# A hybrid decoder trunk on one core: gates and branch outputs with tokens on the partitions, and the modulation sections' sums in the norms' waits

## The chip, the cores and the metric

The kernel runs on 1 core of one Trainium2 chip. The metric is the device time of one execution in microseconds, as the median of several runs. Engines are called TensorE (PE, with its weight loads as PEld), VectorE (DVE), ScalarE (ACT), GpSimd (POOL) and SyncE (SP).

## The reference

256 tokens (T) of 1024 channels (D) pass two layers, in float32. A conditioning vector gives each layer six *sections* of modulation (shift, scale and gate for either half of the layer). Cut to what matters:

```python
mod = (silu(c) @ ada_w[l] + ada_b[l])            # six sections of D
sh1, sc1, g1, sh2, sc2, g2 = jnp.split(mod, 6, axis=-1)
h = rmsnorm(x, norm_mix_w[l]) * (1 + sc1) + sh1
proj = h @ w_in                                   # nine groups of 512, three gates of 1024
y_a = short_conv_mixer(a_b, a_c, a_h, conv_w) @ w_br_a
y_b = hgrn2_mixer(b_q, b_f, b_i, b_g, lb, hgrn_norm_w) @ w_br_b
y_c = chunked_sgu(c_u, c_v, sgu_norm_w, sgu_w, sgu_b) @ w_br_c
merged = sigmoid(gate_a)*y_a + sigmoid(gate_b)*y_b + sigmoid(gate_c)*y_c
x = x + g1 * (merged @ w_o)
h = rmsnorm(x, norm_ffn_w[l]) * (1 + sc2) + sh2
x = x + g2 * (swiglu(h) if l == 0 else top2_of_8_experts(h))
```

A final RMSNorm follows.

## The kernel before, in words

Activations stand with channels on the partitions: `xT`, `hS` (the normed input, split in two), `merged` are 128 x 8 chunks x 256 tokens. Every float32 product is made of three fp32r matmuls. Each operand is split into a high part (a copy rounded to fp32r) and a low part (the rest); high x high, high x low and low x high are added in PSUM (`tile`, L664 is the one matmul call).

**Weights** come in pieces of 512 KB, in the fixed order of the list `PIECES` (`dense_pieces`, L177). SyncE loads piece after piece into `raw`, a ring of 11 slots; a slot is loaded again when VectorE has read it. ScalarE writes the high part of a piece into `split`, a ring of 6 (`high_parts`, L1212), VectorE the low part (`low_parts`, L1447), and TensorE then uses it. Both engines keep some pieces ahead, and each splits the pieces that are due *before* it turns to its next other step: `unit(key)` does so up to a bound, then waits for TensorE's result.

**Sections.** A section is 1024 x 1024 weights, eight pieces that aren't split. VectorE multiplies each with its part of `silu(c)` and adds it into an accumulator (`product`, L1522 and L1525); a product frees its slot of `raw`. TensorE sums the accumulator over the partitions with eight products of one column (`ada_sum`), which is called a section sum, and VectorE adds the bias (`modulate`, L1533). `ADA_ORDER` is the order of the sections, number 6 x layer + part.

**PSUM.** Four banks `psU` go round among the *units* (`UNITS`: one bank each of a projection, gate, branch output), four banks `psA` in pairs among the *events* (`EVENTS`: norm sums, section sums, scores). TensorE opens a unit when the one four before it is emptied, an event when the one two before it is.

**A layer.** Norm 1; the nine groups of projections (`HEAD_GROUPS`) with the recurrence's levels between them; then for each branch, in the order a, c, b: four gate units, four output units. A gate unit holds 2 channel tiles x 256 tokens and takes 48 matmuls of 256 columns with two pieces, an output unit 24 with one. ScalarE takes the sigmoid (L1321) and copies the branch's input into `yS` (high part); VectorE multiplies with the output and adds into `merged` (L1865 to L1871) and makes the low parts. Then the output projection `wo`, the residual add (L1884), and norm 2: ScalarE squares, TensorE sums them over the partitions (`stat_sum`, `stat_pair`), ScalarE takes the root, VectorE the reciprocal (L1559), and chunk after chunk of the next `hS` (L1565, L1276, L1652). In the waits of the norms TensorE does section sums and *fills* (`stream`: products whose result nobody reads, 6 of 256 columns before the dense layer and before layer 1, 2 before the router). Layer 0 goes on with the dense SwiGLU (11 pairs of tiles, then the down product), layer 1 with the router and the experts.

Of the sections, one is summed after branch a in each layer (2 and 8), three in the loop of the dense layer (5, 6, 7), the rest in the norms' waits.

Of the kernel before, what the change touches and what calls it, by code (L numbers as in the profile page):

```python
# [50 lines left out]
BRANCHES = ["a", "c", "b"]  # L51

# [24 lines left out]
ADA_ORDER = [0, 1, 2, 3, 4, 5, 6, 7, 11, 8, 9, 10]  # L77
FFN_ADA = [5, 6, 7]
DOWN_ADA = [11]
# [4 lines left out]
FFN_TAKE = [3, 3, 2] * 3 + [0, 0]  # L84
assert sum(FFN_TAKE) == KD * len(FFN_ADA)

FFN_SUMS = {next(p for p in range(NF // 2) if sum(FFN_TAKE[:p + 1]) >= KD * (n + 1)) + 1: s
            for n, s in enumerate(FFN_ADA)}

# [9 lines left out]
FILL_NORM, FILL_LOGITS = 6, 2  # L99
# [3 lines left out]
def unit_plan():  # L103

    plan = [("c", "D")] + [(("x", j), "A") for j in range(4)] + [(("vec", 0), "A")]
    for l in range(DEPTH):
# [4 lines left out]
        for b in BRANCHES:  # L111
            plan += [((l, "gate" + b, j), "A") for j in range(4)]
            plan += [((l, "y" + b, j), "D") for j in range(4)]
        plan += [((l, "wo", j), "D") for j in range(4)]
        if l == 0:
            plan += [(("ffn", j), "D") for j in range(NF)] + [(("mod", s), "D") for s in DOWN_ADA]
# [6 lines left out]
def event_plan():  # L123

    plan = []
    for l in range(DEPTH):
# [6 lines left out]
        plan += [(("ada", 6 * l + s), "D") for s in (2, 4)]  # L133
        plan += [((l, "norm2"), "A"), (("ada", 6 * l + 3), "D")]
        if l == 0:
            plan += [(("ada", s), "D") for s in FFN_ADA]
            plan += [("down0", "D"), ("down1", "D")]
# [10 lines left out]
def unit_signals():  # L148
# [6 lines left out]
    for key, _ in UNITS:  # L155
# [4 lines left out]
        elif kind in ("i", "v", "ffn"):  # L160
            used += 4 if key[-1] % 2 == 0 else 0
            signal[key] = ("used", used, used)
        elif kind in HEAD_GROUPS or kind in ("gatea", "gateb", "gatec", "wo", "ya", "yb", "yc"):
            used += 1 if kind[0] == "y" else 2
            signal[key] = ("used", used, used)
        else:
            direct += 1
            used += NF if kind == "mod" else 0
# [8 lines left out]
def dense_pieces():  # L177
# [22 lines left out]
    for l in range(DEPTH):  # L200
        for g in HEAD_GROUPS:
# [6 lines left out]
            if g == "f":  # L208
                two = section()
            if g == "f" and l:  # L210
                out += two[:4]
            if g == "ab" and l == 0:
                out[-2:] = two[:2] + out[-2:] + two[2:4]
            if g == "u":
# [7 lines left out]
        out += [("split", "w_o", l, q * 512, 256 * j, 256) for j in range(4) for q in range(2)]  # L222
# [1962 lines left out]
```

## Time and profile before

| | us |
|---|---|
| median of 3 runs (lowest, highest) | 1528.2 (1528.18, 1531.08) |
| the profiled execution | 1528.13 |
| its span in the trace | 1526.2 |
| TensorE busy | 1509.5 (99%) |
| VectorE busy | 1297.7 (85%) |
| ScalarE busy | 958.4 (63%) |

Layer 0's branches lie at about 156 to 264 us of the span, its dense layer at 292 to 489, layer 1's branches at 621 to 729; the experts begin at 768. TensorE's busy time counts pipelined matmuls whose ends are modelled, so 99% says that it seldom stands still, and nothing of how fast it goes; the spacing of matmuls says that. Where TensorE waits, the timeline names the engine that released it.

### The profile page before, as it was taken

How to read it: one execution, taken by the hardware profiler on the slowest of the kernel's cores; microseconds unless marked ns; L12 is line 12 of the kernel's file. 1: busy time of each engine (PE TensorE's matmuls, PEld its weight loads, DVE VectorE, ACT ScalarE, POOL GpSimd, SP SyncE). 2: the span in 40 equal slices, each digit the busy share in tenths (PEclk: the TensorE clock that was granted, in tenths of full speed). 3: DMA queues.
4: the chain of work that ended last, by engine and by line, in shares of the span. 5: the costliest groups of instructions: out<-in, count | busy, mean ns of one | idle time of the engine just before them, and what ended most of it. 6: DMA issues, size and time to landing. Idle time of an engine off the chain costs nothing.

```text
span 1526.2 us, 26183 instructions
## 1 busy us (share of the span) xinstructions
PE 1509.5 (99%) x9449; PEld 1363.4 (89%) x9449; DVE 1297.7 (85%) x1492; ACT 958.4 (63%) x1103; POOL 29.3 (2%) x45
## 2 busy tenths in 40 slices
PE   8999999999999999999999999999999999999997
PEld 7999999999999999999988888888888888888886
DVE  7997788787764788778699999999999999999998
ACT  3535444544543534544498887878878888888785
POOL 0000000000000000000010000000000000000100
PEclk9999999999999999999999999999999999999999
DMA  9946589388996644778389999999999999999993
GB/s 350 332 148 201 187 276 317 111 279 289 367 383 241 208 138 153 239 263 300 110 323 395 410 394 404 381 368 412 366 384 378 379 410 357 393 372 381 410 393 141
DMA packets 228897, 471.01 MB, mean 309 GB/s; under 512 B 16156, under 2 KB 130004, under 8 KB 228820
## 3 DMA queue, kind: packets, MB, share of 16 engines
q1 hardware_dynamic: 225056, 457.27, 82.9%
q0 software_dynamic: 3488, 12.59, 2.1%
q8 instruction: 51, 0.84, 0.2%
q14 instruction: 26, 0.21, 0.0%
q10 hardware_dynamic: 276, 0.09, 0.0%
HBM read 454.69 MB, written 15.21 MB: 308 GB/s over the span
## 4 chain that ended last, share of the span: by engine, by line
PE 94%; DVE 3%; DMA 1%; ACT 0%; issue 0%; SPq 0%; DVEq 0%; ACTq 0%
PE psU L664 68%; PE psA L664 24%; DMA raw<-in_ada_w_dram 1%; DVE split L1954 1%; PE psA L1113 1%; PE psU L1073 0%; PE psU L1026 0%; ACT split L1212 0%; SPq L497 0%; DVE work L1474 0%; DVE work L1484 0%; DVE adacc L1586 0%; DVE adacc L1589 0%; DVE merged L1611 0%; DVE masks L1489 0%
## 5 line engine op out<-in xcount | busy, mean ns | idle before, releaser
L1212 ACT ACTIVATE split<-raw 128x1024 fp32r<-128x1024 f32 x750 | 783.6, 1061 | 358.2 <-PE psU L664 177.3
L1954 DVE TENSOR_TENSOR split<-raw,split 128x1024 fp32r<-128x1024 f32 x528 | 617.0, 1220 | 22.8 <-ACT split L1212 10.6
L664 PE MATMUL psU<-split,yS 128*128 128x512 f32 x2112 | 485.0, 390 | 0.1
L664 PE MATMUL psU<-hS,split 128*128 128x256 f32 x3840 | 470.7, 284 | 2.6 <-DVE hS L1652 2.6
L664 PEld LDWEIGHTS psU<-hS,split 128*128 128x128 f32 x3840 | 464.7, 192 | 4.8 <-DVE split L1447 2.7
L664 PEld LDWEIGHTS psU<-split,yS 128*128 128x128 f32 x2112 | 395.0, 188 | 81.9 <-DVE split L1954 0.7
L1447 DVE TENSOR_TENSOR split<-raw,split 128x1024 fp32r<-128x1024 f32 x222 | 265.0, 1219 | 68.1 <-ACT split L1212 67.4
L664 PE MATMUL psA<-split,hidE 128*128 128x512 f32 x1056 | 246.0, 392 | 0.0
L664 PEld LDWEIGHTS psA<-split,hidE 128*128 128x128 f32 x1056 | 196.4, 188 | 40.2
L1525 DVE SCALAR_TENSOR_TENSOR adacc<-raw,cact,adacc 128x1024 f32<-128x1024 f32 x56 | 71.8, 1282 | 3.6 <-DVE adacc L1525 0.5
L664 PE MATMUL psU<-yS,split 128*128 128x256 f32 x576 | 70.1, 283 | 0.0
L664 PEld LDWEIGHTS psU<-yS,split 128*128 128x128 f32 x576 | 69.6, 192 | 0.0
L664 PE MATMUL psA<-hid_hi,split 128*128 128x256 f32 x352 | 63.9, 284 | 0.3 <-DVE mod L1533 0.3
L664 PEld LDWEIGHTS psA<-hid_hi,split 128*128 128x128 f32 x352 | 55.0, 192 | 0.5 <-DVE mod L1533 0.5
L664 PE MATMUL psU<-split,hS 128*128 128x512 f32 x192 | 45.1, 392 | 0.0
L664 PEld LDWEIGHTS psU<-split,hS 128*128 128x128 f32 x192 | 35.6, 188 | 7.2
L2110 DVE TENSOR_TENSOR hidE<-psA,hidE 128x512 fp32r<-128x512 f32 (+1 forms) x48 | 29.5, 642 | 14.6 <-ACT hidE L1212 14.6
L1321 ACT ACTIVATE sig<-psU 128x512 f32<-128x512 f32 x24 | 14.2, 592 | 38.6 <-PE psU L664 38.6
L1212 ACT ACTIVATE hidE<-psA 128x512 fp32r<-128x512 f32 (+1 forms) x48 | 25.2, 560 | 17.8 <-PE psA L1113 17.8
L664 PE MATMUL psA<-hid,split 128*128 128x256 f32 x128 | 36.2, 283 | 0.0
L2103 DVE TENSOR_TENSOR sig<-sig,psU 128x512 f32<-128x512 f32 (+1 forms) x48 | 29.3, 638 | 6.6 <-PE psU L664 6.6
L664 PE MATMUL psA<-work 128*128 128x128 f32 x272 | 33.3, 275 | 0.0
(255 smaller groups left out, 836.3 us busy)
## 6 DMA issues: line engine op xcount, KB each, us to landing
raw<-in_moe_w_dram SPq DMA_DIRECT2D x496, 512.0 KB, 5.8
raw<-in_w_in_dram SPq DMA_DIRECT2D x116, 512.0 KB, 5.5
raw<-in_ada_w_dram SPq DMA_DIRECT2D x96, 512.0 KB, 7.8
raw<-in_ffn_w_dram SPq DMA_DIRECT2D x66, 512.0 KB, 8.1
raw<-in_moe_w_dram SPq DMA_DIRECT2D x64, 256.0 KB, 6.4
raw<-in_w_o_dram SPq DMA_DIRECT2D x16, 512.0 KB, 8.4
token_rows<-sc SPq DMA_DIRECT2D x11, 512.0 KB, 12.2
raw<-in_w_br_a_dram SPq DMA_DIRECT2D x8, 512.0 KB, 9.2
```

The lines of the kernel that those rows point to most:

```text
L664: return pe.matmul(o, a, b, start=start, stop=stop, skip_group_check=True)
L1113: last = pe.transpose(T_BANKS[g % 2][:, m * CAP:(m + 1) * CAP], sig[0:CAP, 2 + g % 2, m * P:(m + 1) * P], ident[0:CAP, 0:CAP])
L1212: return act.activation(o, i, ACT.Copy)
L1321: act.activation(sig[:, j, :], bank[:, :], ACT.Sigmoid).then_inc(s_uA, 1)
L1447: TTN(split[:, n % SPL, 1, :], raw[:, SPLIT_POS[n] % RAW, :], split[:, n % SPL, 0, :].bitcast(F32), ALU.subtract).then_inc(s_lo, 1)
L1525: STT(acc, raw[:, pos % RAW, :], cact[:, k:k + 1], acc, ALU.mult, ALU.add).then_inc(s_afree, 1)
L1954: TTN(split[:, slot, 1, :], raw[:, (RAW0 + n) % RAW, :], split[:, slot, 0, :].bitcast(F32), ALU.subtract).then_inc(s_lo, 1)
L2103: TTN(sig[0:CAP, 2 + g % 2, 0:width], s, three, ALU.mult).then_inc(s_hrow, 1)
L2110: TTN(h_lo, T_BANKS[g % 2][:, 0:len(tiles) * CAP], h_hi.bitcast(F32), ALU.subtract).then_inc(s_hlo, 1)
```

## The change

Four things. (1) Gates and branch outputs are computed with tokens on the partitions: a unit is 128 tokens x 512 channels, h (or the branch's input) is the stationary operand and the weights are the moving one, 512 columns a matmul (`half_rows`). Two units (the two token tiles) share four pieces for a gate, two for an output, and gate halves and output halves take turns. (2) `merged` then has tokens on the partitions, and TensorE turns it back, 4 x 4 transposes of 128 x 128 (`turn_merged`), before the output projection; ScalarE and VectorE read the turned rows from the spare banks of two events. The branch input for branch a is split earlier, in the head, and for the others when the previous branch's last output is done. (3) Each branch has one section beside it (4, 3, 5 of the layer), the dense loop two (6, 7; two products a pair), the down product one (8), layer 1's head none; three more accumulators. (4) Each norm's wait has three section sums in place of fills (one fill stays before the dense layer), and norm 1 of layer 1 sums the squares on VectorE first, as norm 2 did.

```diff
+WO_ORDER = [(0, 0), (1, 0), (0, 1), (1, 1), (2, 0), (2, 1), (3, 0), (3, 1)]
-ADA_ORDER = [0, 1, 2, 3, 4, 5, 6, 7, 11, 8, 9, 10]
-FFN_ADA = [5, 6, 7]
-DOWN_ADA = [11]
+ADA_ORDER = [0, 1, 2, 4, 3, 5, 6, 7, 8, 10, 9, 11]
+BRANCH_ADA = [4, 3, 5]
+FFN_ADA = [6, 7]
+DOWN_ADA = [8]
+NORM_SUMS = [7, 6, 8]
-FFN_TAKE = [3, 3, 2] * 3 + [0, 0]
+FFN_TAKE = [2] * 8 + [0] * 3
-FILL_NORM, FILL_LOGITS = 6, 2
+FILL_NORM = 1
...
         for b in BRANCHES:
-            plan += [((l, "gate" + b, j), "A") for j in range(4)]
-            plan += [((l, "y" + b, j), "D") for j in range(4)]
+            for hh in range(2):
+                plan += [((l, "gate" + b, 2 * hh + tt), "A") for tt in range(TT)]
+                plan += [((l, "y" + b, 2 * hh + tt), "D") for tt in range(TT)]
...
         for b in BRANCHES:
-            gates = [("split", "w_in", l, q * 512, GATE0[b] + 256 * j, 256) for j in range(4) for q in range(2)]
-            ada = section() if b != BRANCHES[0] else []
-            for q, gate in enumerate(gates):
-                out += [gate] + ada[q:q + 1]
-            out += [("split", "w_br_" + b, l, 0, 256 * j, 256) for j in range(4)]
+            ada = section()
+            for hh in range(2):
+                for q in range(4):
+                    out += [("split", "w_in", l, q * 256, GATE0[b] + 512 * hh, 512)] + ada[4 * hh + q:4 * hh + q + 1]
+                out += [("split", "w_br_" + b, l, q * 256, 512 * hh, 512) for q in range(2)]
...
+            def half_rows(banks, nq, x):
+
+                for q in range(nq):
+                    w = next_split()
+                    for tt in range(TT):
+                        for kk in range(2):
+                            for wp, hp in ((0, 0), (1, 0), (0, 1)):
+                                last = mm(banks[tt][:, :], x[:, hp, 2 * q + kk, tt * P:(tt + 1) * P],
+                                          w[wp][:, kk * 512:(kk + 1) * 512], (q, kk, wp, hp) == (0, 0, 0, 0),
+                                          (q, kk, hp) == (nq - 1, 1, 1))
+                    last.then_inc(s_used, 1)
+
+            def turn_merged(l, i, bank):
+
+                pe.wait_ge(s_mg, 8 * l + 4 + 2 * (i // 2) + 2)
+                if i > 1:
+                    pe.wait_ge(s_ml, 4 * l + i - 1)
...
+                        last = pe.transpose(bank[:, m * T + tt * P:m * T + (tt + 1) * P], row[:, col:col + P], ident[:, :])
...
                 for n, b in enumerate(BRANCHES):
+                    for hh in range(2):
+                        half_rows([open_unit((l, "gate" + b, 2 * hh + tt)) for tt in range(TT)], 4, hS)
+                        if (n, hh) == (2, 1):
+                            stat, spare1 = open_event((l, "norm2"))
+                            scale, spare0 = open_event(("ada", 6 * l + 4))
+                            turn_merged(l, 0, spare0)
+                            turn_merged(l, 1, spare1)
+                        banks = [open_unit((l, "y" + b, 2 * hh + tt)) for tt in range(TT)]
+                        if hh == 0:
                             pe.wait_ge(s_yl, 3 * l + n + 1)
+                        half_rows(banks, 2, yS)
+                    if n == 0 and l == 0:
+                        ada_sum(2)
...
+                        if (j, q, m) == (1, 0, 1):
+                            turn_merged(l, 2, spare0)
+                            turn_merged(l, 3, spare1)
...
-                stat_sum(stat, l)
-                ada_sum(6 * l + 4, scale)
+                stat_sum(stat, 2 * l)
+                ada_sum(6 * l + 4, scale, range(5))
                 stat_pair(stat, 2 * l + 2, 3)
+                ada_sum(6 * l + 4, scale, range(5, KD))
                 ada_sum(6 * l + 3)
+                ada_sum(6 * l + 5)
...
-                    if pair in FFN_SUMS:
-                        ada_sum(FFN_SUMS[pair])
...
-                        stat_pair(stat, 3, 0)
...
+                scale = open_unit(("mod", NORM_SUMS[0]))
+                ada_sum(NORM_SUMS[0], scale, range(5))
+                stat_sum(stat, 1).then_inc(s_used, 1)
+                stat_pair(stat, 3, 3)
+                ada_sum(NORM_SUMS[0], scale, range(5, KD))
+                for s in NORM_SUMS[1:]:
+                    ada_sum(s)
...
+            def branch_high(l, n):
+
+                act.wait_ge(s_y, 3 * l + n + 1)
+                src = {"a": AH, "c": UB, "b": YB}[BRANCHES[n]]
+                copy(yS[:, 0, :, :].rearrange("p a b -> p (a b)"), src).then_inc(s_yh, 1)
...
                 for n, b in enumerate(BRANCHES):
+                    if n:
+                        act.wait_ge(s_used, SIGNAL[l, "y" + BRANCHES[n - 1], 3][1])
+                        branch_high(l, n)
...
+                    gates = SIGNAL[(l, "gate" + BRANCHES[n], 0)][2] - 4
                     for k in ks:
-                        if n:
-                            low_parts(gates + k + 1)
-                        product(6 * l + 2 + n, k)
+                        low_parts(gates + k + (5 if k < 4 else 6))
+                        product(6 * l + BRANCH_ADA[n], k)
...
                     if n:
-                        ada_part(n, range(4))
                         branch_low(n)
-                        ada_part(n, range(4, KD))
+                    ada_part(n, range(4))
                     for j in range(4):
+                        if j == 2:
+                            ada_part(n, range(4, KD))
+                        if (n, j) == (2, 2):
+                            merged_low(0)
+                            merged_low(1)
```

How the order moves on the engines, in three places. First **ScalarE, at the start of branch b in layer 0, before** (`yS` is the branch's input, `split<-raw` the high part of a weight piece, `sig` a gate's sigmoid; `pieceN_loaded` names the slot of `raw`):

```order
L1321 ACTIVATE sig<-psU2 128x512 [waits merged_ready,pieces_used]
L1212 ACTIVATE yS<-work 128x1024 [waits branch_input_ready]
L1212 ACTIVATE split<-raw 128x1024 [waits pieces_used,piece3_loaded]
L1212 ACTIVATE split<-raw 128x1024 [waits pieces_used,piece5_loaded]
L1321 ACTIVATE sig<-psU3 128x512 [waits merged_ready,pieces_used]
```

The same place under the change:

```order
L1244 ACTIVATE yS<-work 128x1024 [waits branch_input_ready,pieces_used]
L1244 ACTIVATE split<-raw 128x1024 [waits pieces_used,piece1_loaded]
L1244 ACTIVATE split<-raw 128x1024 [waits pieces_used,piece3_loaded]
L1244 ACTIVATE split<-raw 128x1024 [waits pieces_used,piece5_loaded]
L1244 ACTIVATE split<-raw 128x1024 [waits pieces_used,piece6_loaded]
L1244 ACTIVATE split<-raw 128x1024 [waits pieces_used,piece7_loaded]
L1244 ACTIVATE split<-raw 128x1024 [waits pieces_used,piece9_loaded]
L1244 ACTIVATE split<-raw 128x1024 [waits pieces_used,piece0_loaded]
L1369 ACTIVATE sig<-psU2 128x512 [waits merged_ready,pieces_used]
L1369 ACTIVATE sig<-psU3 128x512 [waits merged_ready,pieces_used]
```

The branch's input is copied first, and seven pieces (the last two in slots 9 and 0) stand ahead of the two sigmoids, where two stood ahead of the second.

**VectorE, at the same place under the change**, from the last output of branch c on (`sig<-sig,psU` is gate times output, `merged<-merged,sig` the sum, `yS` the low part of the input, `work<-raw,cact` a section product):

```order
L1914 TENSOR_TENSOR sig<-sig,psU 128x512 [waits act_unit_emptied,pieces_used]
L1918 TENSOR_TENSOR merged<-merged,sig 128x512 [waits dve_unit_emptied]
L1857 TENSOR_TENSOR yS<-work,yS 128x1024 [waits branch_input_high]
L1491 TENSOR_TENSOR split<-raw,split 128x1024 [waits act_high_parts]
L1565 TENSOR_SCALAR work<-raw,cact 128x1024 [waits piece9_loaded]
L1491 TENSOR_TENSOR split<-raw,split 128x1024 [waits act_high_parts]
L1568 SCALAR_TENSOR_TENSOR work<-raw,cact,work 128x1024 [waits ada_products,piece0_loaded]
```

The two products read slots 9 and 0, which are loaded again for the last two of ScalarE's seven pieces. Before, the first four products stood ahead of `yS`.

**TensorE, norm 2 of layer 0, before** (`sig,ones` are the sums of squares, `ones,work` and `ones,adacc` section sums, `sgub,ones` fills):

```order
L664 MATMUL psU<-hS,split 128x256 x192
L664 MATMUL psA<-sig,ones 128x256
L664 MATMUL psA<-ones,work 128x1 x8
L664 MATMUL psA<-sig,ones 128x256 x2
L664 MATMUL psA<-ones,adacc 128x1 x8
L664 MATMUL psU<-sgub,ones 128x256 x6
```

And under the change, from the transposes after the last gates of branch b on:

```order
L743 MATMUL psA<-ident,merged 128x128 x8
L672 MATMUL psU<-split,yS 128x512 x24
L672 MATMUL psU<-hS,split 128x256 x36
L743 MATMUL psA<-ident,merged 128x128 x8
L672 MATMUL psU<-hS,split 128x256 x156
L672 MATMUL psA<-sig,ones 128x256
L672 MATMUL psA<-ones,work 128x1 x5
L672 MATMUL psA<-sig,ones 128x256 x2
L672 MATMUL psA<-ones,work 128x1 x3
L672 MATMUL psA<-ones,adacc 128x1 x8
L672 MATMUL psA<-ones,work 128x1 x8
L672 MATMUL psU<-sgub,ones 128x256
```

Eight transposes stand inside the last branch and eight after 36 matmuls of the output projection; the first section sum is cut 5 + 3 around the last squares, and a third sum takes the place of five fills.

## Rows read from the trace of the kernel before

**Rows 1.** The page's chain that ended last: share of the span by engine.
```profile
PE 94%; DVE 3%; DMA 1%; ACT 0%; issue 0%; SPq 0%; DVEq 0%; ACTq 0%
```

**Rows 2.** That chain in order of time: start us, us, what ran.
```profile
107.76 10.89 PE psU L664 x48
...
190.54 1.68 PE psA L664 x16
192.22 72.09 PE psU L664 x600
```

**Rows 3.** Timeline, start of the down product: start, us, engine, operation, idle before.
```profile
424.94 0.36 PE L664 MATMUL psA<-hid_hi,split 128*128 128x256 f32 x1 [0.31 <-DVE mod L1533]
```

**Rows 4.** Timeline, norm 2 of layer 0.
```profile
285.69 0.63 ACT L1266 ACTIVATE sig<-xT 128x512 f32<-128x512 f32 x1 [2.67 <-DVE xT L1884]
...
286.69 0.73 PEld L664 LDWEIGHTS psA<-sig,ones 128*128 128x128 f32 x4
...
287.09 0.17 DVE L1542 SCALAR_TENSOR_TENSOR wm<-mod,vecs 128x8 f32<-128x8 f32 x1
287.45 1.97 PEld L664 LDWEIGHTS psA<-ones,adacc 128*128 128x128 f32 x16
...
288.37 1.75 DVE L1559 RECIPROCAL rstd<-rstd 128x256 f32<-128x256 f32 x1 [1.11 <-ACT rstd L1230]
289.34 2.46 PEld L664 LDWEIGHTS psU<-sgub,ones 128*128 128x128 f32 x12
...
291.96 4.15 PEld L664 LDWEIGHTS psU<-hS,split 128*128 128x128 f32 x31 [0.17 <-DVE hS L1652]
```

**Rows 5.** Timeline, norm 1 of layer 1: sums of the first and the last squares.
```profile
486.09 0.74 PEld L664 LDWEIGHTS psA<-sig,ones 128*128 128x128 f32 x4
...
491.00 0.73 PEld L664 LDWEIGHTS psA<-sig,ones 128*128 128x128 f32 x4 [0.30 <-ACT sig L1266]
```

**Rows 6.** Timeline, norm 2 of layer 1, up to the router's first matmul.
```profile
751.47 0.73 PEld L664 LDWEIGHTS psA<-sig,ones 128*128 128x128 f32 x4
...
754.04 1.38 PEld L1026 LDWEIGHTS psU<-ident,xT 128*128 128x128 f32 x12
...
756.50 3.65 PEld L664 LDWEIGHTS psU<-rtw,merged 128*128 128x128 f32 x32 [0.38 <-ACT merged L1276]
```

**Rows 7.** Timeline, start of branch b in layer 0 (SPq issues the loads).
```profile
228.25 0.75 DVE L1522 TENSOR_SCALAR work<-raw,cact 128x1024 f32<-128x1024 f32 x1
229.03 0.37 SPq L497 DMA_DIRECT2D raw<-in_w_in_dram  x1
...
230.41 0.37 SPq L497 DMA_DIRECT2D raw<-in_w_in_dram  x1
...
232.93 1.06 ACT L1212 ACTIVATE split<-raw 128x1024 fp32r<-128x1024 f32 x1 [4.89 <-DMA raw<-in_w_in_dram]
233.89 0.58 ACT L1321 ACTIVATE sig<-psU 128x512 f32<-128x512 f32 x1
...
236.58 1.06 ACT L1212 ACTIVATE split<-raw 128x1024 fp32r<-128x1024 f32 x1 [1.17 <-DMA raw<-in_w_in_dram]
```

**Rows 8.** Timeline of VectorE: product to product with one low part; multiply to low part.
```profile
206.63 1.28 DVE L1525 SCALAR_TENSOR_TENSOR adacc<-raw,cact,adacc 128x1024 f32<-128x1024 f32 x1
...
208.97 1.28 DVE L1525 SCALAR_TENSOR_TENSOR adacc<-raw,cact,adacc 128x1024 f32<-128x1024 f32 x1
...
259.14 0.68 DVE L1867 TENSOR_TENSOR sig<-sig,psU 128x512 f32<-128x512 f32 x1
...
260.46 0.68 DVE L1851 TENSOR_TENSOR hS<-merged,hS 128x512 fp32r<-128x512 f32 x1
```

**Rows 9.** The page's DMA issues: the longest median landing of raw weights.
```profile
raw<-in_w_br_a_dram SPq DMA_DIRECT2D x8, 512.0 KB, 9.2
```

**Rows 10.** TensorE after its longest stop: timeline, then the stretch's busy times, granted clock.
```profile
41.09 7.17 PE L664 MATMUL psU<-hS,split 128*128 128x256 f32 x45 [2.56 <-DVE hS L1652]
...
41.10:46.00 4.90, 4.90 (x28) 4.90 (x29) 4.88 (x8) 4.41 (x6) 0.00 (x0) 0.65 0.97 283
```

More of the change, by code:

```diff
@@ L167, in unit_signals @@
             direct += 1
[L168 removed]
+            used += NF if key == ("mod", NORM_SUMS[0]) else 0
             signal[key] = ("direct", direct, used)
@@ L452, in program, with accumulator, sum_before @@
         s_yfirst = sem("expert_first_half_ready")
+        def accumulator(s):
+            return accs.get(s, adacc[:, :])
+        def sum_before(s):
+            same = {4: [4, 10], 5: [5, 11], 0: [6], 1: [7]}.get(s % 6 if s not in (6, 7) else s - 6)
+            same = same or [t for t in ADA_ORDER if t != 1 and t not in accs]
+            return same[same.index(s) - 1] if same.index(s) else None
         block = ctx.enter_context(nc.Block())
@@ L712, in project_rows @@
                         yield q // 2
+            def half_rows(banks, nq, x):
[12 more added lines that the diff above has]
+                    pe.wait_ge(s_ml, 4 * l + i - 1)
+                for m in range(2):
+                    col = (2 * i + m) % 4 * P
+                    for tt in range(TT):
+                        row = merged[:, 4 * (i // 2) + 2 * tt:4 * (i // 2) + 2 * tt + 2, :].rearrange("p a b -> p (a b)")
+                        last = pe.transpose(bank[:, m * T + tt * P:m * T + (tt + 1) * P], row[:, col:col + P], ident[:, :])
+                last.then_inc(s_mt, 1)
             def stat_pair(bank, count, j):
@@ L870, in chunk @@
                 def chunk(k):
-                    if l and k == 0:
-                        stream(psU[(units[0] - 1) % 4], FILL_NORM)
                     pe.wait_ge(s_h, 2 * KD * l + k + 1)
@@ L892, in mixer @@
                 for n, b in enumerate(BRANCHES):
-                    for gg in range(2):
-                        for _ in project(lambda j: (l, "gate" + b, 2 * gg + j)):
-                            pass
-                    for j in range(4):
-                        bank = open_unit((l, "y" + b, j))
-                        if j == 0:
-                            pe.wait_ge(s_yl, 3 * l + n + 1)
-                        w = next_split()
-                        for m in range(2):
-                            for k in range(4):
-                                last = tile(bank[:, m * T:(m + 1) * T], w, k, k * 256 + m * P,
-                                            m == 0 and k == 0, k == 3, yS)
-                        last.then_inc(s_used, 1)
-                    if n == 0:
-                        ada_sum(6 * l + 2)
+                    for hh in range(2):
[7 more added lines that the diff above has]
+                        if hh == 0:
+                            pe.wait_ge(s_yl, 3 * l + n + 1)
+                        half_rows(banks, 2, yS)
+                    if n == 0 and l == 0:
+                        ada_sum(2)
                 def chunk_m(k):
@@ L1033, in _ @@
             bank = open_unit("logits")
-            stream(bank, FILL_LOGITS)
             for k in range(KD):
@@ L1514, in product @@
                 dve.wait_ge(s_raw[pos % RAW], 16 * (pos // RAW + 1))
[L1515 removed]
+                acc = accumulator(s)
                 if k == 0:
[L1517 to L1520 removed]
+                    last = sum_before(s)
+                    if last is not None:
+                        dve.wait_ge(*((s_unit, SIGNAL["mod", last][1]) if last in NORM_SUMS else
                                       (s_ev, EVENT_AT[("ada", last) if last else ("half", 1)] + 1)))
@@ L1722, in mixer @@
                     modulate(DOWN_ADA[0])
-                    for k in range(4):
-                        product(6 * l + 2, k)
-                        if k % 2 == 0:
-                            low_parts(SIGNAL[l, "f", 0][2] + 3 + k // 2)
                 else:
@@ L1802, in mixer @@
                 dve.wait_ge(s_eD, emptied(EVENTS, EVENT_AT[(l, "sgu")], "D"))
-                for k in range(4, KD):
-                    product(6 * l + 2, k)
+                for k in range(4, KD) if l == 0 else ():
+                    product(2, k)
                     if k == 5:
@@ L1914, in _ @@
                     for _ in range(FFN_TAKE[pair]):
-                        if done % KD == 0 and done:
-                            modulate(FFN_ADA[done // KD - 1])
                         product(FFN_ADA[done // KD], done % KD)
```

157 lines of the change are left out of this document (77 added, 80 removed).

## The prediction

> **What bounds the kernel now.** I read the chain that ended last first: 94% of the span is TensorE, and the line names only its matmuls with any weight [rows 1]. So an edit counts by what it takes from or adds to TensorE's stream; other engines count only where TensorE would wait for them. Then the chain in order of time, for rates. Narrow matmuls (256 columns) come at 72.09 / 600 = 120.2 ns, wide ones (512) at 10.89 / 48 = 226.9 ns, and one section sum (8 fp32 products of one column, 16 passes) inside the stream costs 1.68 us [rows 2]. Third, the timeline where that stream breaks: the waits before a norm's first result [rows 4 to 6] and the bank wait ahead of the down product, 0.31 us [rows 3]. Last, the hand-over from one branch to the next, because the slots of raw weights, ScalarE and VectorE meet there [rows 7, 8]. Outside these places TensorE never stops.
>
> All sums are against the profiled execution, 1528.13 us (span 1526.2); the median of the runs, 1528.2, is the same number. About 0.2% (3.1 us) is what a measurement of this kernel can tell from no change.
>
> **The change, part by part.**
>
> 1. Wide form. Per layer, 3 branches x (192 + 96) = 864 narrow matmuls become 432 wide ones: 864 x 120.2 = 103.8 us against 432 x 226.9 = 98.0 us, 5.8 us less, so **-11.6 us** for two layers. The weight loads hide under the matmuls in both rates. The wide rate is measured on the same shape (h tile stationary, weights moving), so I take it as it stands. The rows show 12 to 13 ns of cost per matmul beside its columns (2 x 120.2 - 226.9 = 13.5). The Trainium skill, "TensorE: Matmul & The Clock Gate", section "Back-to-back issue gap", puts that fixed part at about 2.5 ns; by it 864 fewer matmuls would give 2.2 us, not 11.6, and the whole sum would be 1530.2. Rows 2 contradict it for this kernel's fp32r matmuls.
>
> 2. Turning the merged rows back. 16 transposes a layer; 12 of this kind load in 1.38 us [rows 6], so 16 x 0.115 = 1.84 us: **+3.7 us** for both layers. The first 8 read banks long finished. The other 8 wait for the last merged sums: after the last branch product VectorE does two pairs of multiply and add (1.32 us each [rows 8]), started 1.3 us late by the weight halves it must do first: ready at 3.95 us. TensorE meanwhile has 36 output-projection matmuls, 4.33 us. Hidden, but with 0.4 us to spare; if the cover fails it costs what VectorE is late. Cost 0, bounds 0 and +2 us a layer.
>
> 3. Sums taken out of the stream. Sections 5, 6, 7 (in the dense layer's loop) and 8 (after the first branch of layer 1) leave it: 4 x 1.68 = **-6.7 us**. The loop's last modulation, for which the down product waited, goes too: **-0.3 us** [rows 3].
>
> 4. The three waits they move into. *Norm 2, layer 0* [rows 4]. T is the load of the last squares' sum. Squares end at 286.32, but T was 286.69, behind a whole section sum; with 5 of its 8 products ahead T is 0.3 us earlier. Then three products follow T by 0.76 us and end near T+1.75, the scale's two small VectorE steps after them, and the reciprocal starts at T+2.15 instead of T+1.68. First result usable 0.47 us later: T+5.74 instead of T+5.27. TensorE: the next sum needs the bank that ScalarE's root empties (T+1.7), two sums at 1.89 (287.45 to 289.34), one fill 0.41: T+5.9. Net **+0.3 us**. *Norm 1, layer 1* [rows 5]: 0.77 us of squares' sums leaves the down product, but the new VectorE sum of squares stands ahead of the last residual add and gives only 0.35 of it back; the reciprocal's 0.4 us delay takes that. **0**; bounds -0.8 and +0.8. *Norm 2, layer 1* [rows 6]: here the router, not a matrix product, follows. Before, its first matmul came at T+5.03. Now TensorE is busy to T+5.48 and then turns 3 tiles (1.38 us): T+6.86, less the 0.3 of T: **+1.5 us**, since routing, gather and the first expert queue up behind it. Bounds 0 (the first expert's splitting hides it) and +1.8.
>
> 5. More sections beside the branches. The queue to follow is ScalarE's. Before, it made two weight halves ahead of a gate's sigmoid at a branch's start; now it makes seven, the last two from slots that VectorE's first and second section product free (the rows of its order under the change). TensorE needs the first gate bank again after six pieces, 72 x 0.227 = 16.3 us. Branch b, times from its first matmul: ScalarE copies the branch input and two halves, done 2.2 and 3.2; VectorE's two low parts to 4.5, its two late pairs for the previous branch (1.32 each) to 7.1, the branch's low part and one more to 9.4, first product 0.75 to 10.2, next low part and product 2.34 to 12.5 [rows 7, 8]. SyncE refills the two slots at 10.2 and 12.5. In rows 7 such refills were usable 3.9 us (first) and 6.2 us (third) after issue; this is the third in its queue with more room, so 4.5: 17.1. Half 1.06, sigmoid 0.58: 18.7. TensorE waits **2.4 us** (1.8 at 3.9, 4.1 at 6.2). Branch c of layer 1: the previous outputs need only the multiply, 1.4 us less, so 1.0 us. Branch c of layer 0: TensorE has the section sum (1.68) first, 0. Branch a has no late outputs: 0. Total 2 x 2.4 + 1.0 = **+5.8 us**; bounds 0 (if VectorE's queue runs 2.4 us ahead of this) and +24 (a landing of 9.2 us [rows 9] each time: 7.1 + 7.1 + 5.7 + 4.1).
>
> Fewer products in the dense loop (2 a pair instead of 3) cost nothing and gain nothing: TensorE does not wait there [rows 1, 2].
>
> Sum: -11.6 + 3.7 - 6.7 - 0.3 + 0.3 + 0 + 1.5 + 5.8 = -7.3: **1520.8 us**.
>
> **Rivals.**
>
> *B, the gates are in time.* Term 5 is 0: 1528.1 - 13.1 = 1515.0. For it: 2.4 us is one or two VectorE instructions of margin in a chain of ten. Against: every link of it has a row.
>
> *C, the clock falls in the norms' waits.* Once in this trace TensorE idled 2.56 us, and the granted clock over the next 4.9 us was 0.65, a mix of 2.4 and 1.2 GHz: 4.9 x 0.35 = 1.7 us lost [rows 10]. Fills held it at 1.00 in the norms; now one-column sums stand there for about 4 us on end. If each wait pays 1.7 us: 1520.8 + 5.1 = 1525.9. Against: before, too, two of the three waits were mostly such sums, and TensorE is seldom idle in them. The Trainium skill, same page, section "What's actually happening", says that the default state is throttled and activity releases it; it does not say whether one column is activity.
>
> *D, slower: the ring of raw weights becomes the bound.* Eight products now stand in all three branches, and all weights pass one ring of 11 slots that VectorE frees in order. If each refill takes the 9.2 us of rows 9 instead of 4.5, TensorE waits 24 us at the four hand-overs: 1528.1 - 13.1 + 24 = 1539. The new time passes the old one once these waits exceed 13.1 us, some 3.3 us each. For it: ScalarE already waited 4.89 us for such a refill. Against: that was with rows of 1 KB; gate and branch weights now come in rows of 2 KB.
>
> *E, the wide form is no cheaper:* one wide matmul takes as long beside the branches as two narrow ones, 240.4 ns, because h and the branch inputs are now the weights that are loaded. Term 1 is 0: 1520.8 + 11.6 = 1532.4. Against: rows 2 show the form with h as weights at 226.9 ns. The page named under 1 points the same way, with its own figure.
>
> **How the numbers follow.** A (forecast) 0.48, with its own range 1517 to 1525; B 0.22; C 0.13; D 0.14, of which half stops short of the full price; E 0.03. Faster by over 0.2% (below 1525.1): A 0.46, B 0.22, C 0.07, D 0.03 = 0.78. Within 0.2%: A 0.02, C 0.06, D 0.05, E 0.01 = 0.14. Slower (above 1531.3): D 0.06, E 0.02 = 0.08. The range 1513.5 to 1527.5 takes B with most of term 4's lower bounds, A and C, and leaves out most of D and E, under 0.2.
>
> **What would show it.** Wide matmuls in the branches at 227 ns; no section sum in the dense loop; 8 + 8 transposes a layer of 0.9 us each without a wait before the second 8; the first residual matmul after norm 2 of layer 0 near T+5.9; the router's first near T+6.9; and at branch b, in both layers, TensorE idle about 2.4 us before the third gate bank, released by a ScalarE sigmoid. No such idle time means B; a granted clock under 1.00 after the norms means C; longer waits at every hand-over with ScalarE waiting for raw weights mean D. I am wrong altogether if a wait appears inside the output projection or if the first expert does not move with the router.

## The result, and the profile after

The changed kernel takes 1547.9 us in the median against 1528.6 us for the kernel before on the same chip: 1.0113 times as long, 95% interval 1.0095 to 1.0132. The forecast was 1520.8, faster. It is slower, by 17 us as the ratio and the two profiled executions have it (19 between the medians), and outside the range.

| | before, us | after, us |
|---|---|---|
| the profiled execution | 1528.13 | 1545.23 |
| its span | 1526.2 | 1543.4 |
| TensorE busy | 1509.5, 9449 matmuls | 1510.5, 8581 matmuls |
| TensorE waiting for ScalarE's sigmoids | 0 | 15.3 |
| mean granted clock | 0.998 | 0.985 |

868 matmuls fewer, and the same busy time: what was saved came back as slow matmuls. The rest is standstill: all of TensorE's waits sum to 25.5 us after the change and to 9.6 before. The three rows of these waits that matter (line, waited for: us in total, times, longest):

```profile
PE psU L672 <- ACT sig L1369: 15.3, 5, 4.1
PE psA L672 <- ACT sig L1298: 0.9, 3, 0.6
PE psU L672 <- DVE hS L1698: 2.6, 1, 2.6
```

L1369 is the gate sigmoid. Nothing like the first row was there before; the third was, with the same 2.6 us. The waits stand in both layers, in branch a (4.11 and 3.91 us), branch b (2.59 and 3.36) and branch c of layer 1 (1.35). TensorE around branch a and branch b of layer 0 (start, us, engine, operation, idle before):

```profile
166.34 5.60 PE L672 MATMUL psU<-split,yS 128*128 128x512 f32 x24
176.06 12.78 PE L672 MATMUL psU<-split,hS 128*128 128x512 f32 x48 [4.11 <-ACT sig L1369]
...
228.60 11.04 PE L672 MATMUL psU<-split,hS 128*128 128x512 f32 x48
239.48 5.60 PE L672 MATMUL psU<-split,yS 128*128 128x512 f32 x24
247.67 12.79 PE L672 MATMUL psU<-split,hS 128*128 128x512 f32 x48 [2.59 <-ACT sig L1369]
260.29 1.03 PE L743 MATMUL psA<-ident,merged 128*128 128x128 f32 x8
```

Two things are to be seen. The 48 wide matmuls take 11.04 us where TensorE comes to them running, and 12.78 behind each of these two stops: such a wait costs 1.7 us more than its length. (Behind the 3.91 us of layer 1 they take 13.65, behind the 1.35 of branch c 11.16.) And the undisturbed 48 come at the forecast rate: (239.48 - 228.60) / 48 = 226.7 ns.

Why the sigmoid of branch a is late, read from the three other queues (SPq issues the loads of raw weights):

```profile
151.38 3.35 DVE L1872 RECIPROCAL work<-work 128x512 f32<-128x512 f32 x1 [1.82 <-ACT work L1262]
...
155.73 3.34 DVE L1874 RECIPROCAL work<-work 128x512 f32<-128x512 f32 x1
...
165.88 0.75 DVE L1565 TENSOR_SCALAR work<-raw,cact 128x1024 f32<-128x1024 f32 x1
```

```profile
166.66 0.37 SPq L505 DMA_DIRECT2D raw<-in_w_in_dram  x1
...
168.05 0.37 SPq L505 DMA_DIRECT2D raw<-in_w_in_dram  x1
```

```profile
158.44 1.06 ACT L1244 ACTIVATE split<-raw 128x1024 fp32r<-128x1024 f32 x1 [1.26 <-PE psU L672]
170.68 1.06 ACT L1244 ACTIVATE split<-raw 128x1024 fp32r<-128x1024 f32 x1 [11.17 <-DMA raw<-in_w_in_dram]
173.93 1.06 ACT L1244 ACTIVATE split<-raw 128x1024 fp32r<-128x1024 f32 x1 [2.19 <-DMA raw<-in_w_in_dram]
174.89 1.06 ACT L1369 ACTIVATE sig<-psU 128x512 f32<-128x512 f32 x2
```

The branch's first matmul was at 155.44. VectorE was still in the mixer's own steps, two reciprocals among them, and began its first section product only at 165.88, 10.4 us in. Layer 1 has the same steps and the same 10.4 us. That product frees the slot for a load issued at 166.66, usable at 170.68; the next, issued at 168.05, is usable at 173.93. ScalarE's order puts both halves ahead of the sigmoid.

Now the clock. Norm 2 of layer 0, which answers to [rows 4]:

```profile
290.51 0.59 PE L672 MATMUL psA<-sig,ones 128*128 128x256 f32 x2
290.94 1.17 PE L672 MATMUL psA<-ones,work 128*128 128x1 f32 x10
292.31 1.13 PE L672 MATMUL psA<-sig,ones 128*128 128x256 f32 x4 [0.19 <-ACT sig L1298]
293.27 0.72 PE L672 MATMUL psA<-ones,work 128*128 128x1 f32 x6
294.09 1.92 PE L672 MATMUL psA<-ones,adacc 128*128 128x1 f32 x16
295.87 3.03 PE L672 MATMUL psA<-ones,work 128*128 128x1 f32 x16
298.76 1.20 PE L672 MATMUL psU<-sgub,ones 128*128 128x256 f32 x2
```

The last section sum takes 3.03 us where the one ahead of it takes 1.92, and the fill's two matmuls 1.20. The windows of the same stretch, and of the router's wait in layer 1 (window, length, busy us and count of PE, PEld, DVE, ACT, POOL; then the granted clock of TensorE, DMA share, GB/s):

```profile
178.00:182.00 4.00, 4.00 (x14) 3.21 (x13) 4.00 (x5) 1.87 (x2) 0.00 (x0) 0.70 0.99 363
182.00:186.00 4.00, 4.00 (x20) 3.29 (x19) 4.00 (x5) 1.87 (x3) 0.00 (x0) 1.00 0.97 327
...
294.00:298.00 4.00, 3.91 (x29) 3.94 (x29) 3.93 (x9) 2.19 (x4) 0.00 (x0) 0.81 0.03 8
298.00:302.00 4.00, 4.00 (x18) 3.82 (x18) 4.00 (x11) 2.55 (x6) 0.00 (x0) 0.50 0.00 0
302.00:306.00 4.00, 4.00 (x31) 4.00 (x31) 2.28 (x5) 1.06 (x1) 0.00 (x0) 0.84 0.00 0
...
770.00:774.00 4.00, 4.00 (x20) 4.00 (x21) 2.94 (x15) 3.28 (x8) 0.00 (x0) 0.50 0.21 76
```

0.50 is the lower level, 1.2 GHz. PE is "busy" 4.00 of 4.00 us there, so the busy column hides the loss; the count does not (18 matmuls in 4 us against 31). From the start to the last matmul, window length times (1 - clock) sums to 20.5 us after and to 1.7 us before. Of the 20.5, 8.5 lie in and behind the sigmoids' waits, 10.2 in and behind the three norms' waits, and 1.7 behind the 2.56 us stop at 41 us, which the kernel before has too. (In every run the clock falls once more after the last matmul, where TensorE has nothing left to do; that is not counted.)

Where the 17.1 us of span came from, in us by stage, each from its first matmul (the first from the span's start) to that of the next:

| stage | before | after | difference | forecast |
|---|---|---|---|---|
| mixer of layer 0, up to norm 2 | 284.58 | 290.51 | +5.9 | -1.6 |
| norm 2's wait | 7.39 | 8.89 | +1.5 | +0.3 |
| dense gate and up products | 132.97 | 128.61 | -4.4 | -5.4 |
| down product and norm 1 | 71.42 | 71.62 | +0.2 | 0 |
| mixer of layer 1 | 253.01 | 262.40 | +9.4 | -2.2 |
| norm 2 of layer 1, up to the router | 7.13 | 11.26 | +4.1 | +1.5 |
| router to the first expert | 11.49 | 11.88 | +0.4 | 0 |
| experts and output | 758.2 | 758.2 | 0 | 0 |

### The profile page after: what moved, and what is told of

Read it like the earlier page. It is cut to its first block and busy times, and to the rows that moved or that the text cites. A ratio compares the mean times of both kernels' runs of the same rounds, so it can differ in the third digit from the quotient of the medians.

```text
span 1543.4 us, 24440 instructions
## 1 busy us (share of the span) xinstructions
PE 1510.5 (98%) x8581; PEld 1328.5 (86%) x8581; DVE 1295.4 (84%) x1495; ACT 956.8 (62%) x1103; POOL 29.2 (2%) x45
## 5 line engine op out<-in xcount | busy, mean ns | idle before, releaser
L2002 DVE TENSOR_TENSOR split<-raw,split 128x1024 fp32r<-128x1024 f32 x528 | 617.2, 1222 | 22.8 <-ACT split L1244 10.4
L672 PE MATMUL psU<-split,yS 128*128 128x512 f32 x2400 | 552.4, 390 | 0.1
L672 PEld LDWEIGHTS psU<-split,yS 128*128 128x128 f32 x2400 | 449.1, 188 | 92.9 <-DVE split L2002 0.7
L672 PE MATMUL psU<-hS,split 128*128 128x256 f32 x2688 | 334.0, 287 | 2.6 <-DVE hS L1698 2.6
L672 PEld LDWEIGHTS psU<-hS,split 128*128 128x128 f32 x2688 | 329.5, 195 | 4.0 <-DVE split L1491 2.7
L672 PE MATMUL psU<-split,hS 128*128 128x512 f32 x768 | 185.8, 403 | 15.3 <-ACT sig L1369 15.3
L672 PEld LDWEIGHTS psU<-split,hS 128*128 128x128 f32 x768 | 148.5, 195 | 48.6 <-ACT sig L1369 17.3
L1957 DVE TENSOR_TENSOR sig<-sig,psU 128x256 f32<-128x256 f32 x22 | 9.1, 418 | 33.8 <-ACT sig L1386 33.8
L1568 DVE SCALAR_TENSOR_TENSOR adacc<-raw,cact,adacc 128x1024 f32<-128x1024 f32 x28 | 35.9, 1281 | 0.7
L1568 DVE SCALAR_TENSOR_TENSOR work<-raw,cact,work 128x1024 f32<-128x1024 f32 x28 | 35.8, 1279 | 0.2
L1386 ACT ACTIVATE sig<-psU 128x256 f32<-128x256 f32 x22 | 8.3, 380 | 41.7 <-PE psU L672 41.7
```

Source lines behind the costliest of these rows:

```text
L672: return pe.matmul(o, a, b, start=start, stop=stop, skip_group_check=True)
L1386: act.activation(sig[:, f % 4, 0:T], bank[:, 0:T], ACT.Silu).then_inc(s_sig, 1)
L1568: STT(acc, raw[:, pos % RAW, :], cact[:, k:k + 1], acc, ALU.mult, ALU.add).then_inc(s_afree, 1)
L1957: TTN(sig[:, f % 4, T:2 * T], sig[:, f % 4, 0:T], bank[:, T:2 * T], ALU.mult).then_inc(s_uD, 1)
L2002: TTN(split[:, slot, 1, :], raw[:, (RAW0 + n) % RAW, :], split[:, slot, 0, :].bitcast(F32), ALU.subtract).then_inc(s_lo, 1)
```

## The experiments

Theory 1: TensorE's waits for the sigmoids, with the clock that each takes down, are one half of the loss. Theory 2: section sums of one column, standing in the norms' waits, let the clock fall, and that is the other half. The rivals stand in the expectations. All ratios are to the kernel before, on the same chip; "us" of gain below are differences of these ratios, and each such difference is good to about 4 us.

| kernel | median, us | ratio (95% interval) |
|---|---|---|
| the change | 1547.9 | 1.0113 (1.0095 to 1.0132) |
| e1_sigmoid_early | 1537.1 | 1.0051 (1.0034 to 1.0069) |
| e2_wide_sums | 1537.7 | 1.0054 (1.0039 to 1.0068) |
| e3_both | 1528.4 | 0.9992 (0.9980 to 1.0004) |
| e4_narrow_fills | 1535.5 | 1.0035 (1.0017 to 1.0053) |
| e6_branch_a_early | 1543.4 | 1.0079 (1.0053 to 1.0104) |
| e5_second_rows_first | 1523.4 | 0.9958 (0.9941 to 0.9974) |
| e8_y_lows_first | 1524.0 | 0.9963 (0.9950 to 0.9977) |

### e1_sigmoid_early

```
# ScalarE, unit(key), gate keys
-    upto = min(upto, SIGNAL[key[0], key[1], 3][2] + 4)
+    upto = used + 3
```

> The changed kernel with one number altered: before the sigmoid of a gate unit ScalarE makes only the split pieces up to three past that unit, no longer seven. Theory (the stalls and the clock they take with them are the loss): no TensorE wait on the sigmoids is left (15.3 us in five places in the changed kernel), the clock rows at 176, 248, 640 and 712 us of the changed kernel are back at 1.00 (8.5 us), the three norm waits stay as they are; 1547.9 - 23.8 = about 1524 us. Rival 1 (pieces made late instead): the splits that now come after the sigmoid reach TensorE late, the stall moves to the weight loads that wait on ScalarE's split, and the time stays at 1540 or above. Rival 2 (the token-major form itself, its transposes or its traffic is what costs): the stalls go and the time stays near 1548.

Measured: 0.0062 of the ratio came back, 9.5 us, not 24. The larger of TensorE's waits:

```profile
PE psA L743 <- DVE merged L1918: 4.0, 2, 2.0
...
PE psU L672 <- DVE split L1491: 2.7, 5, 0.6
...
PE psU L672 <- DVE hS L1893: 1.5, 2, 0.7
```

The sigmoids' 15.3 us are gone, and so are the clock's falls in the branches. In their place stand 8.2 us of other waits: 4.0 ahead of the second transposes, 2.7 on low parts of weights, 1.5 on the merged rows' low parts. The lost time had been hiding lateness of VectorE. So 15.3 - 8.2 = 7.1 us of standstill are gone, and with the falls in the branches 8.5 us of clock. But the fall at the router in layer 1 is now twice as long:

```profile
760.00:768.00 8.00, 8.00 (x40) 8.00 (x39) 1.19 (x12) 0.88 (x2) 0.00 (x0) 0.50 0.00 0
```

The clock's loss up to the last matmul is 15.4 us against 20.5. By stages of the two profiled executions (9.4 us apart), the mixers take 12.2 us less, the norms and the dense layer 0.8 less, and router to first expert 3.6 more (15.46 us against 11.88). (The mixers' 12.2 is some 3 us short of what standstill and clock lost there less; that is not assigned.) Why that fall grew is not shown: the instructions there are the same.

Theory 1 holds in its mechanism and fails in its price: 24 took the standstills as if nothing queued up behind them. Rival 2 is out, since the time did not stay. Rival 1 has a small part of the truth. Three of the five waits on low parts (0.64 us each) go back to ScalarE. The rows are those ahead of TensorE's wait at 226.83; the first wait is for branch c's last product:

```profile
223.51 1.06 ACT L1244 ACTIVATE yS<-work 128x1024 fp32r<-128x1024 f32 x1 [4.35 <-PE psU L672]
...
225.55 3.50 DVE L1491 TENSOR_TENSOR split<-raw,split 128x1024 fp32r<-128x1024 f32 x3 [2.60 <-ACT split L1244]
```

### e2_wide_sums

```
# ada_sum: column k of the bank is the same sum; the columns behind it are overwritten by k + 1, ...
-    last = mm(bank[:, k:k + 1], acc[:, k * P:(k + 1) * P], ones[:, 0:1], True, True)
+    last = mm(bank[:, k:k + P], acc[:, k * P:(k + 1) * P], ones[:, :], True, True)
```

> The changed kernel with every section sum's matmul given a moving operand of 128 columns in place of one (column k of the bank holds the same sum; the loads of weights, which set the pace, stay). Theory (the clock falls in the norms' waits because what stands there is matmuls of one column): granted clock 1.00 in the slices that hold the three norm waits, the same waits in number and order, about 8 to 10 us less; 1538 to 1540 us. Rival (the clock falls because TensorE waits there, whatever the width): slices stay at 0.5 to 0.8, time stays 1548 within 2 us, or more if the wider matmuls take longer than their loads.

Measured: 9.0 us less. Norm 2 of layer 0 and its windows:

```profile
294.93 0.83 PE L672 MATMUL psA<-ones,work 128*128 128x128 f32 x6
295.75 2.02 PE L672 MATMUL psA<-ones,adacc 128*128 128x128 f32 x16
297.61 1.95 PE L672 MATMUL psA<-ones,work 128*128 128x128 f32 x16
299.40 0.60 PE L672 MATMUL psU<-sgub,ones 128*128 128x256 f32 x2
```

```profile
294.00:298.00 4.00, 4.00 (x30) 3.75 (x31) 2.73 (x6) 1.42 (x2) 0.00 (x0) 1.00 0.32 107
298.00:302.00 4.00, 4.00 (x34) 3.90 (x33) 4.00 (x11) 2.69 (x6) 0.00 (x0) 1.00 0.01 2
...
766.00:770.00 4.00, 4.00 (x38) 4.00 (x37) 2.85 (x15) 2.98 (x7) 0.00 (x0) 1.00 0.13 51
```

The same instructions in the same order, 128 columns in place of one: a sum of 16 passes starts 1.86 us ahead of the next instruction instead of 1.78, and the clock stays at 1.00 in all three waits, also in norm 1 of layer 1, where TensorE still stops for 0.56 and 0.53 us. The sigmoids' waits are as they were (16.2 us). Theory 2 is shown, and the rival (TensorE's waiting is what counts, not the width) is out. The two profiled executions are 7.4 us apart, a little less than the ratios.

### e3_both

Both edits.

> Both edits together: no wait on the sigmoids and 128-column section sums. Theory: the two effects are apart and add: 1547.9 - 23.8 - 9 = about 1515 us, below the kernel before. Rival: the two share what they gain, and the time is no better than the better of the two alone (about 1524).

Measured: 0.9992, equal to the kernel before. The two effects add (9.5 + 9.0 = 18.5; measured 0.0121, 18.5 us) as far as 4 us of uncertainty can tell. The level is 13 us above the 1515 written down: the new waits below are 9.7 us, and the clock's two falls in the branches 3.4.

```profile
PE psU L672 <- DVE split L1491: 4.2, 6, 0.9
PE psA L743 <- DVE merged L1918: 4.0, 2, 2.0
...
PE psU L672 <- DVE hS L1893: 1.5, 2, 0.8
```

Its clock still falls twice, behind the 0.8 and 2.0 us waits of each layer. In e1_sigmoid_early the same pairs of waits (0.74 and 2.02, 0.74 and 2.01 us) were followed by no fall, so their length alone does not decide it. In this kernel the norms run at full clock, so it shows term 4 undisturbed: from the first squares' sum to the first residual product 7.5 us in layer 0 (before 7.4), to the router 8.5 in layer 1 (before 7.1).

### e4_narrow_fills

```
# the kernel before, stream(): the fills in the norms' and the router's waits
-    for _ in range(count):
-        mm(bank[:, 0:T], ones[:, :], sgub[:, 0, 0:2, :].rearrange("p g t -> p (g t)"), True, True)
+    for _ in range(2 * count):
+        mm(bank[:, 0:1], ones[:, :], sgub[:, 0, 0, 0:1], True, True)
```

> The kernel before, with the fills that stand in its norms' and router's waits (matmuls of ones against 256 columns, results never read) replaced by twice as many of one column each: about the same time on TensorE, almost no columns. Theory (few columns, not a standstill, is what drops the clock): granted clock below 1.00 in the norm slices at 290, 490 and 755 us, and 4 to 8 us more, 1532 to 1536 us. Rival (one column is as good as 256): clock rows as before, 1528 us.

Measured: 1.0035, 5 us more, inside the 4 to 8 of the theory. TensorE stands still for 8.9 us in all, before 9.6. The fills of norm 2 of layer 0, with what follows them, and the windows of the three places:

```profile
289.94 3.34 PE L664 MATMUL psU<-sgub,ones 128*128 128x1 f32 x24
293.15 7.08 PE L664 MATMUL psU<-hS,split 128*128 128x256 f32 x36
```

```profile
292.00:296.00 4.00, 4.00 (x20) 4.00 (x21) 4.00 (x12) 2.68 (x6) 0.00 (x0) 0.51 0.01 2
...
500.00:504.00 4.00, 4.00 (x23) 4.00 (x22) 4.00 (x12) 2.80 (x6) 0.00 (x0) 0.57 0.00 0
...
764.00:768.00 4.00, 4.00 (x20) 4.00 (x21) 2.12 (x19) 1.48 (x4) 0.00 (x0) 0.50 0.00 0
```

36 narrow matmuls take 7.08 us; at the rate of [rows 2] they take 4.3. (The clock's loss is 11.9 us against 1.7; 1.7 of the difference stand behind the stop at 41 us, where the edit does nothing.) So the old kernel breaks in the same way when its fills lose their columns. What protected it was neither that TensorE stood still less nor the number of its instructions, but the columns of its fills.

### e6_branch_a_early

```
# ScalarE, unit(key), gate keys, in the changed kernel
-    upto = min(upto, SIGNAL[key[0], key[1], 3][2] + 4)
+    upto = used + 3 if key[1] == "gatea" else min(upto, SIGNAL[key[0], key[1], 3][2] + 4)
```

> The changed kernel with the smaller number of split pieces ahead of the sigmoids (three past the unit) in branch a alone; branches c and b as the change has them. Theory (the stop forecast at 0 in branch a is worth its 4.1 + 3.9 us and the clock it drops, 1.7 + 3.4 us): those two stops and the clock rows at 176, 640 and 648 us go; the stops of branch b (2.6 and 3.4) stay; at most 13 us less, 1535 to 1538. Rival (the time lost in branch a gave ScalarE and VectorE the lead that the later branches live on): the later stops grow by what is saved, and the time is above 1542.

Measured: 1.0079, 5 us less than the change (0.5 to 10), and 1543.4 us, which is the rival's time. The waits of branch a are gone (8.0 us), and TensorE's waits for sigmoids sum to 9.3 us in four places:

```profile
PE psU L672 <- ACT sig L1369: 9.3, 4, 3.2
```

Branch c now waits 1.06 and 1.96 us (before this edit 0 and 1.35), branch b 3.15 and 3.15 (2.59 and 3.36), and 1.1 us of waits on low parts are new. So 3.1 of the 8.0 us came back as later waits: that much was lead for the branches behind, and no more. The rest of the rival's time is the clock, and not where the rival looked. The loss in the branches is 6.8 us (8.5 before this edit), but that behind the stop at 41 us is 3.4 instead of 1.7, and that at the router 6.8 instead of 3.4:

```profile
768.00:776.00 8.00, 8.00 (x40) 8.00 (x39) 1.23 (x12) 0.98 (x2) 0.00 (x0) 0.50 0.00 0
```

The edit touches neither place. So this run shows that the stops of branch a are worth about 5 us net of the waits that follow, and leaves the price of their clock open.

### e5_second_rows_first

e3_both, and on ScalarE and VectorE:

```
# ScalarE, before it waits for the previous branch's last product
+    high_parts(SIGNAL[l, "y" + BRANCHES[n - 1], 3][2] + 3)
# VectorE, second half of a branch
-    ada_part(n, range(4, KD))
+    ada_part(n, range(4, 6))
     # branch b: merged_low(0), merged_low(1)
+    ada_part(n, range(6, KD))
# VectorE, unit(key) for the last two outputs of branch b
-    upto = used + AHEAD - 1
+    upto = used + 2
# VectorE, behind branch b's last sum, before merged_low(2)
+    low_parts(SIGNAL[l, "yb", 3][2] + 4)
```

> The kernel with both edits (sigmoids early, 128-column sums), plus an order on ScalarE and VectorE that takes up the waits left in its trace: ScalarE makes three split pieces before it waits to copy the next branch's rows; VectorE makes the first low parts of the merged rows after two section products instead of four, and in branch b's second half makes two low parts of weights less before the last products, and those two behind them. Theory (what is left of the loss in e3 is TensorE's stops in the branches: 0.6 + 0.6 + 0.8 + 2.0 us in layer 0, and 0.7 + 0.6 + 0.6 + 0.8 + 2.0 in layer 1, with 1.7 us of clock after the last of each): the 2.0 us waits on the merged rows and the clock drops at 264 and 728 us go, most of the rest too, 8 to 12 us less; about 1518 us, below the kernel before. Rival (the pieces made later are then late themselves: w_o's third and fourth): stops of 1 to 2 us at the output projection instead, time 1525 to 1529.

Measured: 0.9958 (0.9941 to 0.9974), 1523.4 us. This version is faster than both kernels, the one before by 0.4%. Against e3_both it gives 5 us, not the 8 to 12 of the theory, and the rival's time was not met either; the stops at the output projection are 0.45 us in each layer. The 2.0 us waits on the merged rows and the two falls of the clock are gone, as the theory had it; the clock's loss up to the last matmul is 1.7 us, that of the kernel before. But 7.6 us of short waits are left (9.7 in e3_both):

```profile
PE psU L672 <- DVE split L1492: 6.7, 8, 1.5
...
PE psU L672 <- DVE hS L1894: 0.9, 2, 0.4
```

### e8_y_lows_first

```
# VectorE, second half of a branch, in e5_second_rows_first
-    ada_part(n, range(4, 6))
+    ada_part(n, range(4, 5))
+    low_parts(SIGNAL[l, "y" + b, 3][2])
...
-    ada_part(n, range(6, KD))
+    ada_part(n, range(5, KD))
```

> The kernel e5_second_rows_first with one more step of VectorE moved, in every branch: the low part of the last branch-weight piece before section products 5 to 7, not behind product 5 (and, in branch b, the merged rows' low parts). Theory (the waits of 0.8 + 1.5 us in layer 0 and 0.7 + 1.3 in layer 1 before branch b's last product are VectorE's order): they shrink below 1 us in all, 2 to 3 us less than e5_second_rows_first, about 1520.5. Rival (the raw loads that these low parts need land too late, ScalarE waits 1.5 to 2.5 us for each): the waits stay, and the time stays within 1 us of 1523.4.

Measured: 0.9963, no difference from e5. The waits on low parts shrink from 6.7 to 4.4 us, and 2.1 us of others appear (0.8 for the merged sums, 1.3 that no releaser explains). The time is the rival's, but its waits did not stay as they were: in part they changed place. ScalarE in e5, in branch b of layer 0, waits 1.5 to 3.1 us for each of five raw loads in a row; three of them:

```profile
241.67 1.07 ACT L1244 ACTIVATE split<-raw 128x1024 fp32r<-128x1024 f32 x1 [1.82 <-DMA raw<-in_w_in_dram]
245.19 1.06 ACT L1244 ACTIVATE split<-raw 128x1024 fp32r<-128x1024 f32 x1 [2.45 <-DMA raw<-in_w_in_dram]
248.13 1.06 ACT L1244 ACTIVATE split<-raw 128x1024 fp32r<-128x1024 f32 x1 [1.88 <-DMA raw<-in_w_br_b_dram]
```

That the ring of raw weights is what is left is read from these, and was not tried: it stays open.

## Why the prediction was wrong, by its own steps

**Term 1, wide form, -11.6: right in rate.** The wide matmuls come at 226.7 ns where TensorE runs: 48 in 10.88 us, where 96 narrow ones took 11.54 [rows 2]. Rival E is out. (The term's "12 to 13 ns" beside the columns is 13.5 by its own rows; the sum does not use it.) By the fixed part of 2.5 ns per matmul in the Trainium skill, "TensorE: Matmul & The Clock Gate", section "Back-to-back issue gap", the 48 saved would be worth 0.12 us, not 0.66; the trace after disagrees with it as the one before did. The section gives that figure for an isolated matmul, so using it here was the prediction's own step.

**Term 2, transposes, +3.7: near in size, and free of a wait by luck.** Eight come in 0.8 us, 3.2 in all, and the second eight did not wait. They did not because TensorE had just lost 2.6 us at branch b: with that loss gone (e1_sigmoid_early) they waited 2.0 us a layer, the upper bound that the term gave "if the cover fails". The 0.4 us of margin was none.

**Term 3, sums out of the stream, -6.7 and -0.3: right.** The dense stage gave 4.4 of 5.4 us; what is missing is the clock at its start (302 to 306 us, 0.84). With the clock at 1.00, in e2_wide_sums, the stage takes 127.2 us and gives 5.8.

**Term 4, the norms' waits, +0.3, 0, +1.5: right at full clock, wrong as the kernel ran.** In e3_both they measure +0.1, +0.1 (down product and norm 1, 71.5 us against 71.4) and +1.4. In the changed kernel the first residual product came at T+7.1, not T+5.9, and the router at T+9.5, not T+6.9 (T is the load of the last squares' sum); the clock there was at 0.50.

**Term 5, ScalarE's halves ahead of the sigmoids, +5.8: the step that failed.** The mechanism was right, and its sizes in branch b (2.6 and 3.4 for 2.4) and branch c (0 and 1.35 for 0 and 1.0) were near. In branch b of layer 0 even its links were: first product done 10.2 us in, the later load issued 12.6 us in (forecast 12.5) and usable 4.4 us after (4.5). The sentence "Branch a has no late outputs: 0" was wrong by 8.0 us. I looked for late branch outputs, and what makes VectorE late there is its own mixer steps: its first product was done 11.2 us into the branch, a microsecond later than the 10.2 worked out for branch b. Sum of the term: 15.3. That the halves ahead of the sigmoid make the wait is shown (e1_sigmoid_early, e6_branch_a_early); that the mixer's steps make VectorE late is read from its queue, and no run moved them.

**The clock, costed nowhere in the sum: the second failure.** It was rival C, at 0.13 and 1.7 us a wait. Its objection, that "before, too, two of the three waits were mostly such sums", was the error: e4_narrow_fills shows that the fills among them kept the clock. And the loss behind term 5's own waits was in no case at all, though rows 10 showed just that, a 2.56 us stop followed by 1.7 us of loss. The clock's part of term 5 could have been taken from there, 1.7 us for each stop of that length. In us of the changed kernel the clock is 9.0 in the norms (e2_wide_sums) and, from the durations of the 48 matmuls behind each stop less 11.04, 1.7 + 1.8 + 2.6 + 1.8 = 7.9 in the branches.

The sum with these put in: -7.3 + 9.5 (term 5) + 9.0 + 7.9 = +19.1; measured +17.1 in the profiled execution. The 2 us too many are not assigned.

**Rival D** (the ring) had the right sign and point: slower once the waits pass 13.1 us, and they came to 15.3. Its cause was half right. Loads were usable 4.0 and 5.9 us after issue, not 9.2; they were issued late, and one order of ScalarE made sigmoids wait for them.

## What to carry to other kernels

When an operation is put ahead of another on a queue, work out the moment of its latest input in every place where the order recurs, also where the usual reason for lateness is missing: list what the freeing engine has left to do at that moment. Cost a stop of TensorE with the clock behind it. Do not trust a busy column to say that the clock will stay up: if a wait is filled with useful matmuls of few columns, give them columns, which here cost 0.08 us a sum and brought 9 us. After a stall is removed, expect the next queue's lateness under it: 15.3 us of waits removed gave 9.5, and 5 more were had only by changing the order on two queues once more. And sum the clock stage by stage, for it can move in stages that an edit does not touch.

## What the runs showed of the hardware that I had not expected

- One-column fp32 matmuls stood back to back from 293.27 us on, with TensorE busy nearly all of the time (3.91 and 4.00 of 4 us): the granted clock was 0.81 in 294 to 298 us and 0.50 (1.2 GHz) in 298 to 302. The same instructions with 128 columns left it at 1.00. The cost was 3 us a place (9.0 over three), more than the 1.7 us behind a standstill of 2.6 us.
- In the changed kernel and e6_branch_a_early each stop of 1.96 us or more between matmuls was followed by a fall of the clock (1.96, 2.56, 2.59, 3.15, 3.36, 3.91, 4.11 us), and those of 1.06 and 1.35 us were not. But a stop of 1.74 us in e2_wide_sums and those of 0.74 and 2.02 us in e1_sigmoid_early were not followed by one, while 0.77 and 2.01 us in e3_both were (0.59 at 728 to 732 us in layer 1). Near 2 us the same stop can go either way.
- How long the clock stays down differs for the same instructions: the loss behind the 2.56 us stop at 41 us is 1.7 us in most of the traces and 3.4 in e4_narrow_fills and e6_branch_a_early; that at the router is 3.4 us in the changed kernel and 6.8 in e1_sigmoid_early.
- A section sum whose moving operand is 128 columns of ones costs what one with a single column does, within 5% (1.86 and 1.78 us for 16 passes), in this kernel where each pass loads its own weights.
